# A transformer step on one core: the order of work at the start of layer 0, without filler matmuls and with narrow row sums

## What is computed

```python
def trunk_layer(x, cond, lp, layer, ctx):
    shift1, scale1, gate1, shift2, scale2, gate2 = adaln(cond, lp['w_ada'], lp['b_ada'])
    h = rms_norm(x, lp['norm1_g']) * (1 + scale1) + shift1
    y, own = mixers(h, lp, layer, ctx)
    x = x + gate1 * y
    h2 = rms_norm(x, lp['norm2_g']) * (1 + scale2) + shift2
    x = x + gate2 * hier_moe(h2, lp)
    return x, own
```

## Time and profile before

| | |
|---|---|
| median of 3 runs | 1764.94 us (1764.73 to 1770.18) |
| the profiled execution | 1764.73 us, of which the span is 1762.9 us |
| mean granted clock of PE | 0.986 |
| busy share | PE 92%, DVE 66%, ACT 50%, POOL 27% |
| the chain that ended last | PE 66%, DVE 11%, DMA 8%, ACT 6% |

### The profile page before, as it was taken

The page is one execution under the profiler, slowest core; times in us unless marked ns, Lnnn a source line. Parts: engine busy times, 40 slices in busy tenths (PEclk is TensorE's granted clock), DMA queues, the critical chain, the costliest instruction groups (busy, mean ns, idle before and its releaser), DMA issues.

```text
span 1762.9 us, 33908 instructions
## 1 busy us (share of the span) xinstructions
PE 1623.1 (92%) x13291; PEld 1097.5 (62%) x13291; DVE 1168.7 (66%) x1877; ACT 890.0 (50%) x1477; POOL 471.9 (27%) x448
## 2 busy tenths in 40 slices
PE   6999989999999996998899998999999899879995
PEld 4577766777765565544467886677776655645544
DVE  4594465777635847998676926477774385589974
ACT  4322555666642132877652235466665411358874
POOL 1332252211231212223143324322113311222214
PEclk9999999999999998999999999999999999999998
DMA  9674545532236556899993443232223385479975
GB/s 317 202 263 136 174 138 189 201 111 75 80 108 216 183 198 239 320 404 407 336 313 119 144 135 98 82 102 78 77 75 106 105 272 215 154 281 404 405 307 203
DMA packets 191628, 351.49 MB, mean 199 GB/s; under 512 B 15796, under 2 KB 99315, under 8 KB 191219
## 3 DMA queue, kind: packets, MB, share of 16 engines
q1 hardware_dynamic: 183141, 320.92, 51.6%
q0 software_dynamic: 7776, 28.32, 4.4%
q10 hardware_dynamic: 557, 0.14, 0.0%
HBM read 288.32 MB, written 61.01 MB: 198 GB/s over the span
## 4 chain that ended last, share of the span: by engine, by line
PE 66%; DVE 11%; DMA 8%; ACT 6%; issue 4%; SPq 2%; DVEq 2%; POOL 1%; ACTq 0%; POOLq 0%
PE PS L447 40%; PE PS L454 12%; PE PS L1229 3%; PE PS L1213 3%; DMA y_rows<-scratch 3%; PE PS L987 2%; DMA arena<-in_moe_w 2%; SPq L802 1%; DVE arena L2650 1%; PE PS L947 1%; PE PS L964 1%; ACT arena L1671 1%; DMA wf<-in_moe_w 1%; DMA hpart<-y_rows,wulo 1%; DMA wf<-in_w_out 1%
## 5 line engine op out<-in xcount | busy, mean ns | idle before, releaser
L1963 POOL TENSOR_TENSOR wlo<-wf,whi 128x256 f16<-128x256 f32 (+1 forms) x288 | 296.6, 1063 | 829.7 <-ACT whi L1585 789.8
L447 PE MATMUL PS<-hpart,whi 128*128 128x320 f16 x2048 | 424.1, 300 | 19.0 <-ACT arena L1671 17.8
L447 PE MATMUL PS<-hpart,wlo 128*128 128x320 f16 x1024 | 306.9, 300 | 0.0
L447 PEld LDWEIGHTS PS<-hpart,whi 128*128 128x128 f16 x2048 | 190.3, 98 | 109.0 <-issue 39.8
L447 PE MATMUL PS<-whi,hpart 128*128 128x256 f16 (+1 forms) x1280 | 202.9, 268 | 3.6 <-DVE scratch L2274 3.6
L447 PE MATMUL PS<-wlo,hpart 128*128 128x256 f16 (+1 forms) x640 | 169.3, 268 | 0.0
L447 PE MATMUL PS<-arena 128*128 128x64 f16 (+1 forms) x1944 | 162.2, 234 | 2.4 <-DVE arena L2849 2.4
L2456 DVE TENSOR_REDUCE stat<-PS 128x1 f32<-128x640 f32 (+1 forms) x160 | 110.6, 712 | 80.5 <-PE PS L1213 78.0
L1671 ACT ACTIVATE arena<-PS,pcol 128x320 f32<-128x320 f32 x128 | 67.4, 527 | 169.1 <-PE PS L447 164.0
L454 PE MATMUL PS<-hpart,whi 128*128 128x128 f16 (+1 forms) x768 | 138.0, 303 | 7.9 <-DVE hpart L2128 3.7
L2284 DVE SCALAR_TENSOR_TENSOR scratch<-scratch,cw 128x655 f32<-128x655 f32 x120 | 138.6, 1197 | 4.8 <-issue 0.4
(11 more groups left out here) (375 smaller groups left out, 2923.8 us busy)
## 6 DMA issues: line engine op xcount, KB each, us to landing
arena<-in_moe_w SPq DMA_DIRECT2D x56, 1024.0 KB, 13.3
arena<-in_w_ada SPq DMA_DIRECT2D x48, 1024.0 KB, 8.9
wf<-in_w_gate SPq DMA_DIRECT2D x32, 1024.0 KB, 6.2
wf<-in_moe_w SPq DMA_DIRECT2D x28, 1024.0 KB, 13.8
g_rows<-arena SPq DMA_DIRECT2D x128, 160.0 KB, 1.8
wf<-in_w_in SPq DMA_DIRECT2D x18, 1024.0 KB, 7.8
y_rows<-scratch SPq DMA_DIRECT2D x34, 512.0 KB, 12.8
arena<-g_rows SPq DMA_DIRECT2D x24, 640.0 KB, 4.8
```

What stands on the lines that cost most here:

```text
L447: ins = pe.matmul(out, st, mv, start=first and n == 0, stop=last and n == 2)
L1963: ins = pool.tensor_tensor(lo[:, a:b], wf[j][:, a:b], hi[:, a:b], ALU.subtract)
```

## The change

The work of the first 60 us is ordered anew, and three helpers are edited.

- ACT issues the seven parameter loads right after its row loads; SP no longer does.
- ACT no longer applies the early Silu. It makes its three copies, then the Silu of the condition, then all five squares.
- PE waits for tile 4's copy and for both DVE copies before `params_turn`. The fillers around unit 0 go, and those before the first product are 5 instead of 8. A wait for `rp_ready` stands before the spread (it has been met by then).
- Modulation unit 1 stands before the first product; unit 3 and its turn stand together behind `k` = 3. ACT's copies and its cast of `w_in` unit 1 follow that order.
- POOL splits `w_in` units 0 and 1 in pieces of 1024.
- `lam_sums` becomes the end of `params`, in both layers.
- `sum_tile` multiplies by one column of ones into one column of bank 4 for each tile, and `stds` reads five adjacent columns.

```diff
             in_load(0, 1)
-            params_load(sp, 0)
...
             pe.transpose(PS[:, 1, 0:3 * KC], crow[:, :], ident[0:3 * KC, 0:3 * KC]).then_inc(xt_done.sem, 1)
+            pe.wait_ge(*set_ready(0, 3))
+            pe.wait_ge(*x_copied(0, 3))
+            pe.wait_ge(*x_moved(0, 3))
...
-                    ins = pe.matmul(sums[:, tile, :], sqt[:, tile % 2, k, :], ones[:, :], start=k == 0, stop=k == KC - 1)
+                    ins = pe.matmul(bank(4)[:, tile:tile + 1], sqt[:, tile % 2, k, :], ones[:, 0:1], start=k == 0,
+                                    stop=k == KC - 1)
...
-                    if (layer, u, q) == (0, 0, 0):
-                        idle(3, 4)
...
-            pe.wait_ge(*set_ready(0, 3))
-            pe.wait_ge(*x_copied(0, 2))
             params_turn(0)
-            idle(3, 4)
-            pe.wait_ge(*x_moved(0, 2))
             ada_unit(0, 0)
-            pe.wait_ge(*x_copied(0, 4))
-            pe.wait_ge(*x_moved(0, 3))
             for g in range(4):
                 bands(0, g)
             ada_turn(0, 0)
+            pe.wait_ge(*rp_ready(0, 1))
             spread(0, 0)
             ada_unit(0, 2)
             for g in range(4, 8):
                 bands(0, g)
             ada_turn(0, 2)
-            idle(8)
+            idle(5)
+            ada_unit(0, 1)
...
-                    if l == 0 and k == 0:
-                        ada_unit(0, 1)
                     if l == 0 and k == 1:
                         ada_turn(0, 1)
+                    if l == 0 and k == 3:
                         ada_unit(0, 3)
-                    if l == 0 and k == 2:
                         ada_turn(0, 3)
...
             rows_load(act, 0)
-
-            def square_rows(tile):
-
-                act.wait_ge(*xs_in[tile // 2](0, 32 if tile < 4 else 16))
-                act.activation(sqr[:, tile, :], xtok[:, tile, :], ACT.Square, accum_out=stat[:, 2, tile:tile + 1]
-                               ).then_inc(sq_ready.sem, 1)
-
-            act.wait_ge(*set_ready(0, 1))
-            act.activation(stat[:, 2, 15:16], ones[:, 0:1], ACT.Silu)
+            params_load(act, 0)
             for tile in (0, 2, 4):
                 act.wait_ge(*xt_done(0, tile + 1))
                 ins = act.copy(xT[:, :, tile * P:(tile + 1) * P], PS[:, tile % 4, :].rearrange("p (k n) -> p k n", k=KC))
                 ins.then_inc(x_copied.sem, 1)
-                if tile < 4:
-                    square_rows(tile // 2)
             act.wait_ge(*xt_done(0, TILES + 1))
             act.activation(scf[:, :, :], PS[:, 1, 0:2 * KC].rearrange("p (s k) -> p k s", s=2), ACT.Silu
                            ).then_inc(x_copied.sem, 1)
-            for tile in range(2, TILES):
-                square_rows(tile)
+            for tile in range(TILES):
+                act.activation(sqr[:, tile, :], xtok[:, tile, :], ACT.Square, accum_out=stat[:, 2, tile:tile + 1]
+                               ).then_inc(sq_ready.sem, 1)
...
-                    modulate_one(l, range(4))
+                    modulate_one(l, range(1))
                     ada_copy(0, 1)
+                    modulate_one(l, range(1, 4))
+                    ada_copy(0, 3)
                     in_high(0, 1)
-                    ada_copy(0, 3)
                     modulate_one(l, range(4, KC))
...
-                    low(l * V_ALL + (V_IN + u + 1), u % 2, n=2048 if u < IN_UNITS - 1 else KC * 160,
-                        piece=1024 if l or u > 1 else 256)
+                    low(l * V_ALL + (V_IN + u + 1), u % 2, n=2048 if u < IN_UNITS - 1 else KC * 160)
```

More of the change, by code:

```diff
@@ L300, in build @@
         SEG = [(0, CTX), (CTX, TOK)]
-        sums = PS[:, 2, 0:TILES * P].rearrange("p (t n) -> p t n", t=TILES)
         turned1 = PS[:, 2, 0:860].rearrange("p (t n) -> p t n", t=TILES)
@@ L1543, in stds @@
                     act.wait_ge(*sq_used(l, TILES + KC * n))
-                act.activation(stat[:, 0, 0:TILES], sums[:, :, 0] if l else stat[:, 2, 0:TILES], ACT.Sqrt,
+                act.activation(stat[:, 0, 0:TILES], bank(4, TILES) if l else stat[:, 2, 0:TILES], ACT.Sqrt,
                                bias=epsc[:, :], scale=1.0 / D).then_inc(std_ready.sem, 1)
@@ L2169, in params @@
                 dve.tensor_copy(rp[64:96, :], rpf[64:96, :]).then_inc(rp_ready.sem, 1)
-            def lam_sums(l):
                 dve.wait_ge(*params_in(l, 7 * 16))
@@ L2257, in _ @@
                     norm(l, range(4, KC))
-                    lam_sums(0)
                     lam_last(0)
@@ L2934, in _ @@
                     params(l + 1)
-                    lam_sums(l + 1)
                     for g in range(8):
```

## The result

The changed kernel takes **1784.03 us** (median of 4 runs, 1782.40 to 1785.04), the kernel before, run beside it, 1767.56 (4 runs, 1764.73 to 1771.79). The ratio is 1.0094, 95% interval 1.0075 to 1.0113: **0.9% slower**, 16.5 us where I had forecast 12.4. 1784.03 lies just above the range, whose end was 1784.0. Of the 6.9 us between the forecast of 1777.1 and 1784.03, 4.1 are cost; the other 2.8 are the starting value: the sum began at 1764.73, the fastest of four executions of the kernel before whose median is 1767.56. Three executions (one each of the changed kernel, of e7 and of e12, at 2390 to 2822 us and a mean granted clock of 0.55 to 0.66) were in a slower state and are in no median and no ratio. The profiled execution took 1782.78, its span is 1781.0 (before 1762.9), and TensorE's mean granted clock is 0.971 (before 0.986).

A forecast was written before the change was run, and what follows sets the result against it. TensorE, busy 92% of the span, was taken to set the pace. Start 4.3, slow clock afterwards 0.4, transfers 1.2 and layer boundary 6.5 sum to 12.4; on 1764.73 that gives 1777.1 us, eight-in-ten range 1767.5 to 1784.

The forecast's parts named there:

- PE waits until 20.85 ... the spread starts there, 29.0: +2.5.: Layer 0 start: PE waits for Silu and DVE's copies; ACT's later chain moves the spread from 26.46 to 29.0.
- Start: the transfers: Parameter loads on ACT's queue run beside the rows of x and delay PE's first transposes: 0 to 2.7, taken 1.2.
- So the lambda sums cost nothing; without that cover they would cost 0.65.: Layer 0 start: DVE finishes params with the lambda sums by 26.5 and waits for the Sqrt, so they cost 0.
- Spread and unit 2 lose about 1.7: unit 2 ends at 33.9.: Layer 0 start, fillers removed: clock at 1.2 GHz under the spread; loss 1.7, bounds 0 and 3.2.
- rival (c): Start stays at 1.2 GHz from 22 into the products; unit 2 ends at 36.1, total 1785; chance 10%.
- POOL now works in 1024-column pieces ... I take 5.2, ready at 41.6.: Before the first product: POOL's split takes 5.2 against 5.56, gain 0.1 to 1.4; first product at 41.6 against 37.85.
- The hole grows from 2.2 to 3.8 us.: Ahead of the fifth product block: PE waits 3.8 for DVE and ACT work; block at 56.5 against 52.23, +4.3.
- Afterwards ... it may stay low longer, I take 0.4.: After the hole ahead of the fifth block: clock may stay low longer, 0 to 1.7, taken 0.4.
- The layer boundary: One-column sums let the clock fall to 1.2 GHz from about 896; worked out 7.5, range 4.5 to 8.1, taken 6.5.
- (a): Clock holds at both start and boundary; start costs 2.6, boundary -0.5, total 1766.8; chance 10%.
- (b): Clock falls at the start but holds at the boundary; 5.9 - 0.5, total 1770.1; chance 13%.
- (d): Boundary's one-column sums cost by columns; three on the chain save 5.2, clock held, total 1762.1; chance 5%.

The follow-up runs named there:

- e7: Kernel before with only the layer 1 sums of squares narrowed from 128 columns to one; 1776.62 us against 1768.37, ratio 1.0049.
- e12: Kernel before with unit 1 ahead of the first product, unit 3 behind the first block, its turn behind the second; 1765.79 us against 1769.14, ratio 0.9978.
- e1: Changed kernel with layer 1's sums of squares 128 columns wide again; 1776.62 us, ratio to the kernel before 1.0047.
- e5: Changed kernel with the parameter loads back on SP's queue and lam_sums back at its old place; ratio to the kernel before 1.0081.
- e2: Changed kernel with two filler matmuls of 256 columns ahead of layer 1's second, third and fourth one-column sum tiles; ratio to the kernel before 1.0089.
- e13: Changed kernel with four filler matmuls of 256 columns ahead of layer 1's second, third and fourth one-column sum tiles; ratio to the kernel before 1.0092.
- e9: Changed kernel with ACT's start as before: early Silu of a constant, two squares between copies, three behind the Silu; ratio to the kernel before 1.0090.
- e10: Changed kernel with the edits of e9 and e5 together; ratio to the kernel before 1.0068.
- e4: Changed kernel with POOL's pieces for w_in units 0 and 1 back at 256 columns instead of 1024; ratio to the kernel before 1.0089.
- e8: Kernel before with only POOL's pieces for the first units of w_in lengthened from 256 to 1024 columns; ratio 0.9994.

## Why the prediction was wrong, step by step

The sign, the places and the mechanism of the larger term were right. The sizes were not: the boundary cost 9.4 instead of 6.5 (8.2 in the medians of e7), and the start 10.5 in the profiled pair instead of 5.9, but 7.6 to 7.8 in the median of e1 and between the means of the traces with the same start. The 3.7 us that came back behind the boundary are scatter and hid a part of it. The steps that failed are the size of the boundary, the growth of the hole ahead of the fifth block, and a path into the spread that was followed on ACT alone.

- **"The copy ends at about 19.06, the load at 20.34, Silu at 20.55."** Right in kind (load at 19.90, Silu at 21.19). The load before the first copy that I had named as a sign against me was there too, in idle time, and cost nothing in this trace.
- **"PE waits until 20.85 ... the spread starts there, 29.0: +2.5."** It started at 30.60. ACT's copy of unit 0 ended at 28.65 and not 28.05, as x landed 0.66 later; the bands, held by the landing of `w_ada` at 25.17, ended another 0.3 later; and the turn took 1.87 at 1.2 GHz where I had allowed 0.95. I had let the clock fall only under the spread. That landing was missed: the step "Start: the transfers" put the parameters' bytes ahead of x, and not ahead of `w_ada`. By itself it moved little, as e5 shows, since ACT's chain was as long.
- **"So the lambda sums cost nothing; without that cover they would cost 0.65."** In the changed kernel's trace they did. I had not counted that they wait for the parameter loads, and in e1 this wait came last and cost PE 1.08.
- **"On the path between 0 and 2.7 ...: I take 1.2."** Not borne out by itself: e5, with the loads back, has its first product at 43.69, and e1, e2 and e13, without, at 43.60 to 43.79. Only with ACT's chain short does it show: 1.5 from e9 to e10 (41.17, 39.63), the place of the lambda sums included. The rule that I had quoted, the Trainium skill, "DMA: Bandwidth & Descriptors", Issuing engines are not separate DMA queues, is borne out by e5: the bytes held up a load of SP's from ACT's queue.
- **"Spread and unit 2 lose about 1.7: unit 2 ends at 33.9."** They lost 2.8 (6.05 us from the spread's start to 36.65, against 3.25), and the bands and the turn before them ran at half speed too. That is near the bound of 3.2 that I named and the first half of my rival (c), "unit 2 ends at 36.1"; its second half, fillers and unit 1 at half speed, did not come.
- **"POOL now works in 1024-column pieces ... I take 5.2, ready at 41.6."** Failed. POOL took 4.23, quicker than my value, and the first product gained 0.1, the lower end of what I had allowed: DVE was held by POOL. I treated the piece as POOL's own matter.
- **"The hole grows from 2.2 to 3.8 us."** It was 5.63 in PE's timeline. The 3.8 us of DVE and ACT work became 5.6: 1.0 by the long pieces, 0.8 by the fact that POOL splits unit 1 at that time at all (e4, e8). The rest of this step held: 11.25 from first product to the end of the turn, where I had 11.1.
- **"Afterwards ... it may stay low longer, I take 0.4."** 22.54 for the 144 matmuls against 21.42, 1.1: inside my 0 to 1.7.
- **The layer boundary: "I expect 1.2 GHz from about 896 ... I take 6.5."** The mechanism was right and is shown by e1 and e7; this term was mis-sized. The clock fell 3.1 us into the sums (907.0), where I had it 4.4 us in, and stayed low for 23.9 us, to 930.9, where I had 18. So four sum tiles ran slowly instead of the three that I counted, at 3.41 to 3.50 instead of 3.2: unit 4 started 7.1 later against the first sum than before, not 5.4. Unit 4 and the spread at 1.2 GHz added 2.4 (I had 2.1). The full working of that step gave 7.5, and my 6.5 was taken off it for a later fall that did not come. With 9.4 the upper bound of 8.1 was too low too.
- **The rivals**: (a), (b) and (d) are refuted by the windows at 0.50 and by a tile of 1.95 us at full clock. The copies moved on ACT cost nothing visible.

What stays open: what set the time in the upper half of e2's runs, what the place of the lambda sums and the queue of the loads are worth apart, and why the clock came back at 918.6 in e7 and only at 930.9 in the changed kernel.

## What to carry to other kernels

A matmul that looks wastefully wide may be what holds the clock: here five groups of 128 columns, made one column wide, saved 0.1 us each and cost 9.4 us around them, and filler matmuls put in their place did not bring it back reliably. Before costing a reordering, follow every chain that ends in the same wait, the loads too: of two equal chains shortening one gives nothing. Before reading a microsecond out of one trace, see how far two traces of the same code lie apart: here it was up to 2.8 us at the first product. And look at which operations of VectorE lie beside a GpSimd operation before making that one longer.

## What the runs showed of the hardware

- TensorE can be busy in 23.00 of 23 us and be granted 1.2 GHz throughout: the work was four sum tiles of 16 one-column matmuls with their weight loads, transposes, four filler records, and at the end 16 records of 512 columns. In e2 4 more records of 256 columns ahead of each of three tiles went with 2.4 GHz throughout in the profiled run.
- A one-column fp32 tile of 16 records takes 1.84 to 1.95 us at 2.4 GHz and 3.41 to 3.50 at 1.2 GHz; with 128 columns it takes 1.95 to 2.05 at 2.4 GHz. The columns cost nearly nothing; the 16 weight loads beside the tile at 903.89 take 1.86 of its 1.95 us.
- A VectorE operation on 8 columns with two inputs in SBUF took 1.82 us beside a GpSimd piece of 2.13 us, and 0.37 or 0.38 beside pieces of 256 columns.
- Where no activation stood before it, ScalarE's first PSUM copy had a table load of its own ahead of it (1.28 us at 10.76 in the changed kernel), besides those before Silu and Sqrt.
